# Four expert score steps computed between the gate groups, scores ahead of products, and the loads in another order

## The reference

```python
scores = jnp.einsum('thpd,hpkd->thpk', qh, sub_keys)
s_top, i_top = lax.top_k(scores, PEER_TOPK)
...
best, pos = lax.top_k(cand.reshape(T, PEER_HEADS, -1), PEER_TOPK)
gate = jax.nn.softmax(best, axis=-1)
...
act = jax.nn.gelu(jnp.einsum('td,thkd->thk', tb, expert_u[ib]))
return jnp.einsum('thk,thkd->td', gb * act, expert_v[ib])
```

## Time and profile before

| | us |
|---|---|
| median of 3 runs | 3798.36 (3797.69 to 3798.58) |
| span of the profiled execution, first to last instruction | 3797.1 |
| steps of layer 0, first score to end of last product | 718.2 to 1924.4 |
| steps of layer 1, first score to end of last product | 2574.6 to 3778.7 |
| TensorE busy in the whole span | 3605.6 (95%) |
| DVE busy in the whole span | 2667.4 (70%) |
| DMA, mean over the span | 294 GB/s |

### The profile page before, as it was taken

The page is one execution under the profiler, slowest core; times in us unless marked ns, Lnnn a source line. Parts: engine busy times, 40 slices in busy tenths (PEclk is TensorE's granted clock), DMA queues, the critical chain, the costliest instruction groups (busy, mean ns, idle before and its releaser), DMA issues. The chain is left out here.

```text
span 3797.1 us, 45352 instructions
## 1 busy us (share of the span) xinstructions
PE 3605.6 (95%) x15346; PEld 2481.3 (65%) x15346; DVE 2667.4 (70%) x5705; ACT 628.9 (17%) x1536; POOL 1894.8 (50%) x1593
## 2 busy tenths in 40 slices
PE   7999997899999999999989999879999999999998
PEld 3445576667666766666655456776776667666666
DVE  4424598887878667666665356898878777676667
ACT  3212216510000000000021231281000000000000
POOL 0011029866676566666501100597566755666663
PEclk8999999999999999999999999999999999999999
DMA  9711206999999999999951022199999999999997
GB/s 395 293 58 53 100 25 112 275 386 401 403 408 408 356 408 401 408 408 408 382 200 40 28 76 77 40 162 368 378 406 406 408 390 380 408 404 408 408 408 280
DMA packets 496520, 1116.54 MB, mean 294 GB/s; under 512 B 201360, under 2 KB 240400, under 8 KB 495104
## 3 DMA queue, kind: packets, MB, share of 16 engines
q0 software_dynamic: 175104, 637.61, 42.5%
q1 hardware_dynamic: 316768, 463.63, 35.5%
q10 hardware_dynamic: 4512, 13.76, 1.0%
HBM read 1068.68 MB, written 46.12 MB: 294 GB/s over the span
## 5 line engine op out<-in xcount | busy, mean ns | idle before, releaser
L1501 PE MATMUL ps<-big,y_nat 128*128 128x336 f32 x4096 | 1216.6, 450 | 54.6 <-DMA y_nat<-in_peer_ut 46.8
L1501 PEld LDWEIGHTS ps<-big,y_nat 128*128 128x128 f32 x4096 | 761.6, 190 | 438.8 <-issue 100.4
L2102 POOL DMA_INDIRECT big<-in_peer_u,gates_area x608 | 769.4, 1265 | 460.4 <-DVE kn_area L1888 286.6
L2113 POOL DMA_INDIRECT big<-in_peer_v,gates_area x608 | 690.9, 1136 | 416.0 <-DVE big L1906 269.6
L1906 DVE SCALAR_TENSOR_TENSOR big<-big,kn_area 128x1024 f32<-128x1024 f32 x608 | 785.4, 1292 | 7.0 <-DVE big L1906 0.5
L1888 DVE CUSTOM_DVE_ANT_0 big<-big,y_nat 128x1024 f32<-128x1024 f32 x608 | 739.7, 1223 | 1.3
L1616 ACT ACTIVATE gates_area<-ps 128x336 f32<-128x336 f32 x256 | 115.2, 450 | 2034.7 <-PE ps L1501 2034.7
L1514 PEld LDWEIGHTS ps<-gates_area,y_nat 128*128 128x128 f32 x2048 | 363.7, 190 | 61.2 <-issue 61.2
L1514 PEld LDWEIGHTS ps<-gates_area,big 128*128 128x128 f32 x2048 | 363.7, 190 | 61.2 <-issue 61.2
L1514 PE MATMUL ps<-gates_area,big 128*128 128x208 f32 x2048 | 381.0, 339 | 0.0
L1514 PE MATMUL ps<-gates_area,y_nat 128*128 128x208 f32 x2048 | 381.0, 339 | 0.0
(11 more groups left out here) (294 smaller groups left out, 3388.8 us busy)
## 6 DMA issues: line engine op xcount, KB each, us to landing
y_nat<-in_peer_ut SPq DMA_DIRECT2D x256, 512.0 KB, 8.4
y_nat<-in_peer_v SPq DMA_DIRECT2D x128, 512.0 KB, 6.7
big<-in_peer_v SPq DMA_DIRECT2D x128, 512.0 KB
big<-in_w_mod SPq DMA_DIRECT2D x24, 2048.0 KB, 13.4
expert_gates<-big SPq DMA_DIRECT2D x8, 4096.0 KB, 22.2
gates_area<-expert_gates SPq DMA_DIRECT2D x128, 136.0 KB, 9.5
kn_area<-expert_gates SPq DMA_DIRECT2D x128, 136.0 KB, 9.9
big<-in_w_in SPq DMA_DIRECT2D x8, 2048.0 KB, 15.6
```

Source lines behind the costliest of these rows:

```text
L1501: last = pe.matmul(ps[:, 6 + par, 0:NX], u_s[par][:, k, :], h_t[:, k, X0:ND], start=(k == 0), stop=(k == KD - 1))
L2102: pool.indirect_dma_start(out=u_ring[:, k % USLOTS, :], out_offset=None, in_=io["peer_u"][:, :], in_offset=bass.IndirectOffsetOnAxis(ap=ro ...
L2113: pool.indirect_dma_start(out=v_ring[:, k % VSLOTS, :], out_offset=None, in_=io["peer_v"][:, :], in_offset=bass.IndirectOffsetOnAxis(ap=ro ...
```

## The change

- S(0) to S(3) move into the gate groups: one of the 8 products of a score after each group, S(0) after groups 3 to 10, S(1) after 11 to 18, S(2) after 22 to 29, S(3) after 30 to 37, counted from 0 (`early_scores`). They write to banks 4 to 7. u(2) and u(3) are loaded between the stores of the gates.
- In the steps TensorE begins with P(0) and then does S(j), P(j-3): the scores run three places further ahead of their products than one step.
- SP issues the loads in another order: u(i+6), v(i+3), g(i+5), with the same waits for free buffers as before.
- Gelu reads banks 4 to 7 for the first four steps. DVE and POOL are as before.

```diff
+EARLY = 4
+EARLY_AT = (3, 11, 22, 30)
...
-                    def follow(j, par, past):
-
-                        u, g, v = stream(sp, j, par)
-                        sp.wait_ge(s_a, past)
-                        u()
-                        sp.wait_ge(s_h, past)
-                        g()
-                        sp.wait_ge(s_g2, past)
-                        v()
+                    def keys_for(j, par):
+
+                        sp.wait_ge(s_a, j - 1)
+                        stream(sp, j, par)[0]()
+
+                    def gates_for(j, par):
+
+                        sp.wait_ge(s_h, j - 1)
+                        stream(sp, j, par)[1]()
+
+                    def values_for(j, par):
+
+                        sp.wait_ge(s_g2, j - 1)
+                        stream(sp, j, par)[2]()
...
+                            if (i, half) in ((1, 0), (1, 1)):
+                                keys_for(2 + half, half)
                             sp.wait_ge(s_fe, 16 * i + 8 * (half + 1) - SKIPPED)
                             store(i, half)
...
-                    with sp.Fori(0, N_KEYS // 2 - 1) as m:
+                    keys_for(4, 0)
+                    keys_for(5, 1)
+                    gates_for(2, 0)
+                    gates_for(3, 1)
+                    values_for(2, 0)
+                    gates_for(4, 0)
+                    with sp.Fori(0, (N_KEYS - 6) // 2) as m:
                         for par in range(2):
-                            follow(2 + 2 * m + par, par, 1 + 2 * m + par)
+                            keys_for(6 + 2 * m + par, par)
+                            values_for(3 + 2 * m + par, 1 - par)
+                            gates_for(5 + 2 * m + par, 1 - par)
+                    values_for(N_KEYS - 3, 1)
+                    gates_for(N_KEYS - 1, 1)
+                    values_for(N_KEYS - 2, 0)
+                    values_for(N_KEYS - 1, 1)
...
+                    def early_scores(j, k):
+
+                        if k == 0:
+                            pe.wait_ge(s_us[j % 2], 16 * (j // 2 + 1))
+                            if j >= 2:
+                                pe.wait_ge(s_ce, DENSE)
+                        last = pe.matmul(ps[:, 4 + j, 0:NX], u_s[j % 2][:, k, :], h_t[:, k, X0:ND], start=(k == 0), stop=(k == KD - 1))
+                        if k == KD - 1:
+                            last.then_inc(s_a, 1)
...
                         last.then_inc(s_f, 1)
+                        for j in range(EARLY):
+                            if 0 <= n - EARLY_AT[j] < KD:
+                                early_scores(j, n - EARLY_AT[j])
...
-                    scores(0, 16, 1)
-                    scores(1, 16, 2)
+                    pe.wait_ge(s_ge, 4)
                     products(0, 16, 1, first=True)
-                    with pe.Fori(0, N_KEYS // 2 - 1) as m:
-                        scores(0, 16 * (m + 2), 4 * m + 2)
+                    with pe.Fori(0, N_KEYS // 2 - 2) as m:
+                        scores(0, 16 * (m + 3), 4 * m + 6)
                         products(1, 16 * (m + 1), 2 * m + 2)
-                        scores(1, 16 * (m + 2), 4 * m + 4)
+                        scores(1, 16 * (m + 3), 4 * m + 8)
                         products(0, 16 * (m + 2), 2 * m + 3)
+                    products(1, 16 * (N_KEYS // 2 - 1), N_KEYS - 2)
+                    products(0, 16 * (N_KEYS // 2), N_KEYS - 1)
                     products(1, 16 * (N_KEYS // 2), N_KEYS, last_step=True)
...
-                        act.activation(gelu_s[par], ps[:, 6 + par, 0:NX], ACT.Gelu_apprx_tanh).then_inc(s_ge, 1)
+                        act.activation(gelu_s[par], ps[:, 4 + j if j < EARLY else 6 + par, 0:NX], ACT.Gelu_apprx_tanh).then_inc(s_ge, 1)
```

## The result

The changed kernel takes 3772.76 us (median of four runs, 3765.36 to 3778.93), the kernel before, run beside it, 3798.03 (3796.61 to 3798.58). The ratio is 0.9929, 95% interval 0.9916 to 0.9943: 25 us faster by the medians, 27 by the ratio, where I had forecast 58. The direction was right and the time lies in the range of 8 in 10, but less than half of the gain came.

A forecast was written before the change was run, and what follows sets the result against it. The DMA's bytes at 408 GB/s were taken to bound the steps. Per layer 24.1 + 2.6 + 4.3 - 2 = 29.0 us, 58 for two layers, gave 3740 us, with an 8 in 10 range of 3714 to 3778.

The forecast's parts named there:

- TensorE's saved scores: Four scores taken off the steps, 18.1 us of TensorE's work a layer; not counted as a term of the gain.
- The wait for u: TensorE's idle time before every second score in the steps, 1.33 us at most places; predicted to go.
- rival B: Steps: 408 GB/s is the loads' own pace, not a ceiling, so TensorE sets the time; 3694 us, chance 0.06.
- the debt: Full steps: TensorE's pace leaves 0.28 us of DMA work behind per step; rings absorb it, light steps pay it.
- the start of P(0): Start of the steps: about 1.6 us won, 2 to 4 lost after some 9 us of TensorE idle; counted as nothing.
- Of the 30.1 us I leave 6 unused: Steps: of the DMA's 30.1 us unused time a layer, 6 stay; gain 24.1 us a layer.
- the end, 4.3 us: End of a layer: last landing to last product shrinks from 10.7 to 6.4 us; gain 4.3 us.
- the gate groups, 2 us: Gate groups: score products and u loads between them cost 2 us a layer, between 0 and 4.
- The loads of u(2) and u(3), 2.6 us: Steps: moving 2 x 524 KB of loads into the gate groups shortens the stretch by 2.6 us a layer.
- A: Steps: the DMA stays as uneven as it is; 3792 us with all idle time left, 3758 with half; chance 0.24.
- C: Steps: ACT's gelu, behind late dots, becomes the bound; TensorE stands 2 us at 38 places; 3816 us, chance 0.07.
- D: Gate groups: u(2), u(3) come late behind the stores, TensorE stalls, the steps' gain is lost; 3798 us, chance 0.05.

The follow-up runs named there:

- e1: Changed kernel with all four early scores S(0) to S(3) behind the last gate group instead of between the groups; 3776.62 us, ratio 0.9937.
- e5: Changed kernel with ACT doing gelu(j+1) before it waits for the dots of step j; 3774.38 us, ratio 0.9931.
- e10: Changed kernel with e6 and e5 together, and VectorE's h(j+1) ahead of the rows of step j in the last eight steps; 3772.98 us, ratio 0.9936.
- e2: Kernel before with only S(0) and S(1) moved between its gate groups, loads in their old order; 3820.07 us, ratio 1.0046.
- e11: Changed kernel with S(2) and S(3) behind the last gate group, loads of u(2) and u(3) still between the stores; 3771.11 us, ratio 0.993.
- e14: e1 with the load of v(0) issued between two gate stores; 3775.74 us, ratio 0.9931.
- e3: Kernel before with gathered rows loaded to, and dots done on, only 64 of the 128 partitions; 4084.02 us, ratio 1.0758.
- h2: Changed kernel with row gathers after each buffer's first bringing 2 KB half rows to all 128 partitions; 3701.11 us, ratio 0.974.
- e6: Changed kernel with v(126) and v(127) loaded into the two u buffers right behind the last scores; 3775.79 us, ratio 0.9936.

## Why less than half of the forecast gain came

**What held.** The new order makes the gain, by letting the DMA be full; TensorE's saved scores are no term of it (e1). The wait for u goes. 408 GB/s is the ceiling of this kernel's loads, in every full slice of the variants that load whole rows, so rival B was rightly put low. (By that, the 435 GB/s of the Trainium skill, "DMA: Bandwidth & Descriptors", Specifications, is not reached in any run here.) Full steps run at 9.05 us, thirty in a row, while the rings take up the debt, and the start of P(0) is worth about nothing: the gap is 8.4 us against the 9 of idle time I named.

**The first step that failed: "Of the 30.1 us I leave 6 unused".** Measured in layer 1: 14.7, so 15.4 us recovered instead of 24.1; in layer 0 about 16, by the same sum over its stretch (33 to 17: 473.70 MB in 719.7 to 1913.7 before, 473.22 in 726.1 to 1903.2 after). I took the idle time of a layer as one number, where it was three. Of the 30.1, 20.1 lay in the middle, where the lead can fill them, and 10.0 at the two ends, where it can't: at the start the row transfers and the loads of the steps only set in, at the end the last unit's 16 adds are spread over three steps and little is left to load. Of the middle, 15 of 20 came back, and e5 and e10 show that the other five are worth nothing: filled, they come back at the end, because the last unit still needs its 28 to 31 us behind its weights.

**The second: the end, 4.3 us.** It measured 1.8: last landing to last product went from 10.7 to 8.9 instead of 6.4 (in layer 0 to 8.1). "At the end the last rows' adds stand before W(127) on DVE" misread the kernel before. Its adds were done at 3768.95, and W(127) then waited for its gelu:

```profile
3770.30 0.51 DVE L1876 TENSOR_TENSOR gates_area<-gates_area,kn_area 128x336 f32<-128x336 f32 x1 [1.35 <-ACT gates_area L1616]
```

What ended last there was u(127), S(127), P(126), P(127). After the change I counted one add, h(127) and P(127), and overlooked that three products stand in a row with two v buffers. And the last product is not the only thing that ends a layer: e10 has it ten us earlier and takes the same time, by way of the last add.

**The third: the gate groups, 2 us.** They measured 5.3 and 9.2, and 3.8 to 9.2 over all kernels with the same groups. That "a TensorE that is 0.565 us later in its own gap does not slow it" (POOL) is wrong, at 1 to 2.3 us for a score of eight products, and more in e2 and in layer 0 of e11. The part I did charge for sure, a load between the stores, costs nothing (e14).

**The loads of u(2) and u(3), 2.6 us,** measured 2.4: the stretch moved 473.08 MB instead of 474.06 (1.2 in layer 0; other small loads fall in or out at the edges).

Sum for layer 1: 15.4 + 2.4 + 1.8 - 5.3 = 14.3, measured 14.0. For layer 0: 15.7 + 1.2 + 2.6 - 9.2 = 10.3, measured 10.6. Twice 29 was forecast; 10.6 and 14.0, with 2.7 elsewhere, were found. (Of the 9.2 us, 5 are the slower rhythm that the profiled run happened to have; e5 has 113.5 us there.)

**The rivals.** The time lies in A's band (3752 to 3792). Half of the idle time did stay, as in its 3758, but not for its reason: the light stretches filled, and full steps ran at 9.05 us. C's path appeared as described, 12 times instead of 38, and earned nothing when it was taken away (e5); my reading is that a stand of TensorE gives the DMA the time it is short of. D did not happen as described, but the gate groups, where it lay, took back 5.3 of what layer 1 won elsewhere (19.3) and 9.2 of layer 0's 19.8.

## What to carry to other kernels

When a transfer rate is the bound, split its idle time by place before you promise any of it: here a longer lead filled idle time in the middle and none at the two ends, where the buffers are not yet full or the last dependent chain runs out at the program's own spacing. Where two paths end almost together, removing one shows the other and gains nothing. A standstill whose name changes when you remove its cause, at the same total, is the bound seen from elsewhere; halving the bytes told what renaming waits could not. "Free" work between instructions of a tightly coupled rhythm of four engines is to be priced by a run, even where each engine shows a gap.

## What the runs showed of the hardware

- Row transfers to 64 of 128 partitions kept the DMA share at 0.99 while only 235 GB/s were moved (e3); 2 KB pieces to all 128 partitions moved 248 GB/s at a share of 0.78, with TensorE as the bound (h2).
- A DMA issue on SP right behind a gate store took 16 to 20 us instead of 0.33 (2481.66 and 2504.92 in the kernel after, 2481.20 in e14, where the groups took their usual 110.1 us):

```profile
2481.66 15.86 SPq L1329 DMA_DIRECT2D y_nat<-in_peer_ut  x1
2504.92 17.57 SPq L1329 DMA_DIRECT2D y_nat<-in_peer_ut  x1
```

- A stand of TensorE can cost a second time: the first part of a product, 1.88 us, took 3.75 behind 8.36 us of idle time and 3.75 behind 6.03 (e6), 2.87 behind 3.10, 1.98 behind 2.07 (after, layer 0) and 1.95 behind 0.68 (e6).
- Two scores a layer, moved from the gap ahead of P(0) to a place between the gate groups, made the kernel before 0.46% slower (e2).
